# Spreading the expert weights: both halves of a weight in one 256-column matmul, summed by VectorE

## The reference, cut to what matters

```
s = einsum('nhpd,hpkd->nhpk', qry, sub_keys)
s_top, i_top = top_k(s, 16)
sc, ci = top_k(s_top[:, :, 0, :, None] + s_top[:, :, 1, None, :], 16)
experts = e_a * 128 + e_b          # e_a, e_b: the picked pair of key numbers
gw = softmax(sc)
out = sum over the picks of  gw * gelu(u[expert] . x) * v[expert]
```

## Time and profile before

| | us |
|---|---|
| median of 3 runs | 3646.55 (3645.39 to 3648.05) |
| the profiled execution, its own time | 3648.54 |
| its span, first to last instruction | 3646.8 |
| TensorE busy over the span | 3294.8 (90%) |
| VectorE busy | 1940.5 (53%) |
| ScalarE busy | 1114.6 (31%) |
| GpSimd busy | 1142.1 (31%) |
| mean granted TensorE clock | 0.939 |

### The profile page before, as it was taken

The page is one execution under the profiler, slowest core; times in us unless marked ns, Lnnn a source line. Parts: engine busy times, 40 slices in busy tenths (PEclk is TensorE's granted clock), DMA queues, the critical chain, the costliest instruction groups (busy, mean ns, idle before and its releaser), DMA issues. The chain is left out here.

```text
span 3646.8 us, 38847 instructions
## 1 busy us (share of the span) xinstructions
PE 3294.8 (90%) x15129; PEld 1668.3 (46%) x15390; DVE 1940.5 (53%) x2816; ACT 1114.6 (31%) x1609; POOL 1142.1 (31%) x545
## 2 busy tenths in 40 slices
PE   8678889999979899999999999999988877589897
PEld 3333347544644545464664444444433434234443
DVE  4772767543234675867770455555555442339631
ACT  3232234343323233342433333232333121232321
POOL 3311330133513243424223443444423001024332
PEclk9889999999989999999999999999999776599999
DMA  4101210122312244756577655565521000012321
GB/s 146 41 29 47 98 64 1 55 90 99 126 47 93 92 154 136 208 154 190 151 197 212 222 203 204 200 207 200 204 85 66 0 24 23 23 58 93 102 97 67
DMA packets 262822, 411.22 MB, mean 113 GB/s; under 512 B 146736, under 2 KB 146928, under 8 KB 262256
## 3 DMA queue, kind: packets, MB, share of 16 engines
q1 hardware_dynamic: 262640, 408.72, 34.3%
HBM read 339.45 MB, written 69.21 MB: 112 GB/s over the span
## 5 line engine op out<-in xcount | busy, mean ns | idle before, releaser
L498 POOL TENSOR_TENSOR weights_lo<-weights_as_loaded,weights_hi 128x1024 bf16<-128x1024 f32 x507 | 1112.5, 2196 | 2337.0 <-ACT weights_hi L494 2336.9
L494 ACT ACTIVATE weights_hi<-weights_as_loaded 128x1024 bf16<-128x1024 f32 x507 | 533.7, 1054 | 1185.2 <-PE banks L434 604.6
L1768 DVE TENSOR_TENSOR activation_lo<-activation_f,activation_hi 128x512 bf16<-128x512 f32 x128 | 278.9, 2179 | 313.0 <-ACT activation_hi L1660 313.0
L434 PE MATMUL banks<-normed_lo,weights_hi 128*128 128x512 bf16 x930 | 359.4, 386 | 27.0 <-PEq L296 15.8
L1581 PE MATMUL banks<-normed_hi,weights_hi 128*128 128x512 bf16 x991 | 376.6, 380 | 7.8 <-ACT gelu_out L1646 6.6
L1629 PE MATMUL banks<-activation_hi,weights_hi 128*128 128x512 bf16 x1004 | 380.8, 379 | 1.1
L1629 PE MATMUL banks<-activation_hi,weights_lo 128*128 128x512 bf16 x1003 | 380.4, 379 | 1.1
L1629 PE MATMUL banks<-activation_lo,weights_hi 128*128 128x512 bf16 x1003 | 380.4, 379 | 1.0
L1581 PE MATMUL banks<-normed_lo,weights_hi 128*128 128x512 bf16 x999 | 378.8, 379 | 1.7
L1581 PE MATMUL banks<-normed_hi,weights_lo 128*128 128x512 bf16 x1000 | 379.2, 379 | 1.3
L434 PE MATMUL banks<-normed_hi,weights_hi 128*128 128x512 bf16 x912 | 352.0, 386 | 29.5 <-PEq L277 20.2
(11 more groups left out here) (431 smaller groups left out, 4833.1 us busy)
## 6 DMA issues: line engine op xcount, KB each, us to landing
weights_as_loaded<-in_u_tiles SPq DMA_DIRECT2D x128, 512.0 KB, 3.9
weights_as_loaded<-in_v_tiles SPq DMA_DIRECT2D x128, 512.0 KB, 3.5
gelu_of_dots<-gelu_out SPq DMA_DIRECT2D x128, 256.0 KB, 2.2
activation_f<-gelu_of_dots SPq DMA_DIRECT2D x128, 256.0 KB, 3.7
expert_weight<-expert_weights SPq DMA_DIRECT2D x128, 256.0 KB, 4.0
expert_weights<-weight_grid_even SPq DMA_DIRECT2D x32, 512.0 KB, 5.9
expert_weights<-weight_grid_odd SPq DMA_DIRECT2D x32, 512.0 KB, 6.5
weights_as_loaded<-in_w_xbc SPq DMA_DIRECT2D x24, 512.0 KB, 3.5
```

Of the source, the lines that this page charges most:

```text
L434: ins = nc.tensor.matmul(self.ps[:, b, 0:tok], wk[:, s, k * P:(k + 1) * P], x[xk][:, g * 8 + k, :], start=first, stop=last)
L494: self.nc.scalar.activation(self.whi[:, s, :], self.wraw[:, s, :], ACT.Copy).then_inc(self.w_hi[s], 1)
L498: self.nc.gpsimd.tensor_tensor(self.wlo[:, s, :], self.wraw[:, s, :], self.whi[:, s, :], ALU.subtract).then_inc(self.w_lo[s], 1)
L1768: nc.vector.tensor_tensor(glo[:, j, :], gf[:, j, :], ghi[:, j, :], ALU.subtract).then_inc(S["g_lo"], 1)
```

## The change

One matmul of 256 columns makes both halves of a token. Its result is two runs of 128 in PSUM, which are no longer added up there. ScalarE copies the high run to the grid, and VectorE adds the low run to it (a new function `move` on VectorE, which signals `moved`; ScalarE now signals `hi_moved`). A group now fills all four banks, so `spread(g)` waits for the move of group g-1, half by half. `hotB` takes the layout of `hotA`, four tokens innermost, so its 128 key numbers lie 8 bytes apart as well. Groups follow as one, one, two over three slots in place of one, two over two; a block takes 12 slots in place of 11.

```
-    SPREAD_FROM = (30, 57, 85, 97)
-    TURN_AFTER = (22, 49, 76, 93)
-    EXP_AFTER = (13, 29, 57, 84)
+    SPREAD_FROM = (30, 58, 86, 98)
+    TURN_AFTER = (22, 52, 79, 95)
+    EXP_AFTER = (13, 29, 58, 86)
...
-                after[n] = min(left, 1 + n % 2)
+                after[n] = min(left, 1 + (n % 3 == 2))
...
-        hotB = self.sb("one_hot_b", [P, 2, G, P], BF16, ctx=tmp)
+        hotB = self.sb("one_hot_b", [P, 2, 2, P, 4], BF16, ctx=tmp)
-        hotAs = [self.sb("weighted_hot_a_" + n, [P, 2, 2, P, 4], BF16, ctx=tmp) for n in ("hi", "lo")]
+        hotAw = self.sb("weighted_hot_a", [P, 2, 2, 2, P, 4], BF16, ctx=tmp)
...
+        def halves(i):
+            return self.ps[:, 4 + 2 * i:6 + 2 * i, :].rearrange("p b (t w a) -> p (b t) w a", w=2, a=P)
...
                 def spread(g):
-                    if g < 2:
+                    if g == 0:
                         pe.wait_ge(S["copied"], TT)
-                    else:
-                        pe.wait_ge(S["moved"], 2 * (g - 1))
                     pe.wait_ge(S["hot"], g + 1)
                     for i in range(2):
+                        if g:
+                            pe.wait_ge(S["moved"], 2 * (g - 1) + i + 1)
                         for n in range(4):
-                            for m in range(2):
-                                ins = nc.tensor.matmul(self.ps[:, 4 + g % 2 * 2 + i, n * P:(n + 1) * P],
-                                                       hotB[:, g % 2, 4 * i + n, :], hotAs[m][:, g % 2, i, :, n],
-                                                       start=m == 0, stop=m == 1)
+                            ins = nc.tensor.matmul(self.ps[:, 4 + 2 * i + n // 2, n % 2 * 2 * P:(n % 2 + 1) * 2 * P].rearrange(
+                                                       "p (w a) -> p w a", a=P),
+                                                   hotB[:, g % 2, i, :, n], hotAw[:, g % 2, i, :, :, n], start=True, stop=True)
                         ins.then_inc(S["spread"], 1)
...
-                        nc.scalar.activation(grid[lap % 2][:, :, at + 4 * i:at + 4 * i + 4],
-                                             self.ps[:, 4 + g % 2 * 2 + i, :].rearrange("p (t a) -> p a t", a=P),
-                                             ACT.Copy).then_inc(S["moved"], 1)
+                        nc.scalar.activation(grid[lap % 2][:, :, at + 4 * i:at + 4 * i + 4].rearrange("p a t -> p t a"),
+                                             halves(i)[:, :, 0, :], ACT.Copy).then_inc(S["hi_moved"], 1)
...
+                def move(g):
+                    lap, at = g // 8, g % 8 * G
+                    for i in range(2):
+                        dve.wait_ge(S["hi_moved"], 2 * g + i + 1)
+                        cells = grid[lap % 2][:, :, at + 4 * i:at + 4 * i + 4].rearrange("p a t -> p t a")
+                        nc.vector.tensor_tensor(cells, cells, halves(i)[:, :, 1, :], ALU.add).then_inc(S["moved"], 1)
...
                     for k in range(PER):
                         one_hots(t, k)
+                        if k:
+                            move(t * PER + k - 1)
                         if t == 2 and k == PER // 2:
                             weigh_picks(3)
+                    move(t * PER + PER - 1)
```

More of the change, by code:

```diff
@@ L1494, in peer @@
         tot = self.sb("weight_sums", [P, PH], ctx=tmp)
-        iota_b = self.sb("iota", [P, P], BF16, ctx=tmp)
         iota_4 = self.sb("iota_fourfold", [P, P, 4], BF16, ctx=tmp)
@@ L1511, in peer @@
         S = {n: self.sem("peer_" + n) for n in ("keys", "scored", "copied", "shifted", "exped", "weights", "turned", "taken",
-                                               "hot", "spread", "moved", "weighed", "g_hi", "g_lo", "summed", "zeroed")}
+                                               "hot", "spread", "hi_moved", "moved", "weighed", "g_hi", "g_lo", "summed", "zeroed")}
         act_stored = [self.sem(f"gelu_stored{j}") for j in range(2)]
@@ L1750, in one_hots @@
                         dve.wait_ge(S["spread"], 2 * (g - 1))
-                    nc.vector.tensor_tensor(hotB[:, g % 2, :, :], iota_b[:, :].unsqueeze(1).to_broadcast((P, G, P)),
-                                            col[:, k * G:(k + 1) * G].unsqueeze(2).to_broadcast((P, G, P)), ALU.is_equal)
+                    nc.vector.tensor_tensor(hotB[:, g % 2, :, :, :], iota_4[:, :, :].unsqueeze(1).to_broadcast((P, 2, P, 4)),
+                                            four(col, k), ALU.is_equal)
                     link(nc.vector.tensor_tensor(hotA[:, :, :, :], iota_4[:, :, :].unsqueeze(1).to_broadcast((P, 2, P, 4)),
                                                  four(row, k), ALU.is_equal))
-                    nc.vector.tensor_tensor(hotAs[0][:, g % 2, :, :, :], hotA[:, :, :, :], four(whi, k), ALU.mult)
-                    link(nc.vector.tensor_tensor(hotAs[1][:, g % 2, :, :, :], hotA[:, :, :, :], four(wlo, k), ALU.mult))
+                    nc.vector.tensor_tensor(hotAw[:, g % 2, :, 0, :, :], hotA[:, :, :, :], four(whi, k), ALU.mult)
+                    link(nc.vector.tensor_tensor(hotAw[:, g % 2, :, 1, :, :], hotA[:, :, :, :], four(wlo, k), ALU.mult))
                     nc.vector.memset(spacer[:, :], 0.0).then_inc(S["hot"], 1)
+                def move(g):
[4 more added lines that the diff above has]
+                        nc.vector.tensor_tensor(cells, cells, halves(i)[:, :, 1, :], ALU.add).then_inc(S["moved"], 1)
                 def weigh(n):
@@ L1770, in _ @@
                 iota = self.consts[:, C_IOTA:C_IOTA + P]
-                nc.vector.tensor_copy(iota_b[:, :], iota)
                 link(nc.vector.tensor_copy(iota_4[:, :, :], iota.unsqueeze(2).to_broadcast((P, P, 4))))
```

## The result

The changed kernel takes 3736.8 us in the median of four runs (3734.3 to 3739.9), the kernel before 3647.0 beside it: a ratio of 1.0247, with an interval from 1.0229 to 1.0265. The forecast was 3688 with a range from 3650 to 3735. The direction was right, the size was half of what came, and the time lies just above the range. The profiled span grew from 3646.8 to 3732.5 us, and the mean granted clock fell from 0.939 to 0.927. Times are those of executions in the chip's usual state; one execution of run 1's kernel, its profiled one, ran at a mean granted clock of 0.562, took 5749.9 us and stands in no comparison.

What follows compares the result with a forecast made beforehand. TensorE's instructions bound the retrieval layer's first phase. -2 + 19 + 15 + 6 + 3 = +41 us on the profiled 3648.5 gives 3689.5, and 3688 as that run lay 2.0 above the median; range 3650 to 3735.

Steps and rivals of the forecast that it cites:

- the saving: TensorE's spread matmuls over 64 groups: 0 to 4.5 us less, taken as 2.
- a price of the columns' distance: Spread matmuls: 128 columns 8 bytes apart take the array 0.115 us, twice what contiguous ones take.
- The strided load: Weight load of `hotB`, now strided: even if twice as long, hidden under a matmul's 0.22 us, cost nothing.
- the new wait: Second group of a double slot waits for the first's moves, released by VectorE's addition: 16 x 1.2 = 19 us.
- The six late loads: Double slots 38, 65, 68, 95, 101, 107: late weight tiles delay ScalarE's moves, 6 x 2.4 = 15 us.
- the last block's start: Around slot 98, VectorE's one-hots and addition come late at the block boundary: 3 us (1 to 5).
- B: Spread matmuls: columns not slow, 256 take 0.109 us, kernel not slower: 3640 (3625 to 3652); chance 15%.
- C: Double slots: the wait doesn't bite as moves and second group's matmuls overlap better: 3645 to 3655; chance 5%.
- price of copy and addition: Moves in a double slot: ScalarE's first half 0.60 us, VectorE's additions 0.69 each, second group starting at 3.01.
- Rival A: Grid moves: addition or copy slow at 256 bytes between elements; 3706 at twice 0.69, 3761 at 2.18; chance 18%.
- The clock: TensorE at half clock after idle stretches of about 3.4 us, seven places, four counted: 6 us (0 to 11).
- off the path: VectorE's one-hots and additions, stretched where they meet GpSimd, fit beside TensorE's slots except at block starts.

Runs made afterwards that it cites:

- run 1: Changed kernel with ScalarE's copy and VectorE's addition walking the grid in runs of four neighbouring tokens: 3705.3 us, 1.016 of the kernel before.
- run 5: Kernel before with two tokens innermost in the moving operand, its columns 4 bytes apart in place of 8: 3599.3 us, 0.9869.
- run 6: Kernel before with only `hotB`, the stationary operand, in the change's layout, columns 8 bytes apart: 3653.0 us, 1.0014.
- run 4: Changed kernel with ScalarE's copies put ahead of its rounding of the next weight tile: 3703.2 us, 1.014.
- run 1 again: Second run, for a profile, of the changed kernel with copy and addition in runs of four tokens: 3710.6 us.
- run 10: Joined form: changed kernel with both spread operands 4 bytes apart, copy and addition in runs of four, copies ahead of rounding: 3618.8 us, 0.9917.

## Why the prediction came out half as large

**Right.** TensorE bounds the phase, and what is put between its instructions counts in full (86.1 us came up in this phase, 85.7 over the whole span). 256 columns take 0.229 us, forecast from 0.222 to 0.231, and the saving was 1.6 us, forecast 2. That rested on reading a price of the columns' distance out of the earlier trace rows against the earlier trace rows; run 5 confirms it. The strided load is hidden (run 6). The place and the releaser of the new wait are those named. The six late loads cost 17.3 us against 15, at the slots named, and the last block's start 3.7 against 3. Single slots lasted 7.0. Rivals B and C are out: the matmuls came 0.229 us apart and not 0.109, and the double slots waited.

**The step that failed** is the price of copy and addition under "The new wait": "ScalarE's first half ends at 1.64 + 0.60" and "0.69 each". Both were taken from rows in which the engine walks contiguous elements or runs of four, while the diff turns that walk round. Rival A named the cause and half of the price. It doubled the addition alone and got 3706; ScalarE's copy doubled too. With 1.07 and 1.29 the prediction's own sum gives 1.64 + 1.07 + 1.29 + 0.06 = 4.06 for the start of the second group, against the 4.12 measured, and with it 2.5 us a double slot in place of 1.2. Rival A's argument against itself, "no such price on ScalarE's writes", came from writes of four neighbours, which say nothing on single ones. Run 1 shows that the order alone makes the difference. The Trainium skill ("SBUF — State Buffer", Specifications (TRN2)) wants two hits in a memory line of 16 bytes for full bandwidth. These rows agree: 256 bytes apart is one hit and cost 1.8 to 1.9 times as much, runs of 16 bytes cost nothing.

**The clock** was the second miss, 23 us against 6. I counted places with about 3.4 us of idle time, since 1.51 had left the clock at 1.00 in the earlier trace rows. Stalls of 2.1 us were enough, and they stand in every double slot, so the price is not that of seven places but of sixteen. In part it grows with the first miss: with 1.62 us (run 4) the next slot took 7.5 to 9.1 nearly everywhere. But it was a miss of its own too. The prediction let a stall of its own length, about 1.1 us, cost nothing, and in run 1 again, which has that stall, the next slot was slower behind five of the seven undelayed double slots, up to 8.7. The clock as slot 32's second group starts, and behind it (columns as in the earlier trace rows):

```profile
1411.30:1412.30 1.00, 0.96 (x5) 0.55 (x6) 1.00 (x2) 0.00 (x0) 0.89 (x1) 0.99 1.01 369
1412.30:1415.70 3.40, 3.40 (x12) 1.29 (x11) 3.32 (x7) 1.19 (x2) 0.00 (x0) 0.50 0.05 16
```

In the joined form of run 10, with idle times of 1.08 us, the next slot kept its 6.09 everywhere. So the length of the idle time alone does not decide, and what else does stays open.

**Missed** altogether were slots 41 and 86, 4.7 us together. ScalarE in slot 86, then VectorE in slot 41:

```profile
1792.72 1.28 ACT L1672 ACT_TABLE_LOAD   x1
1794.01 0.31 ACT L1672 ACTIVATE picked<-picked 128x128 f32<-128x128 f32 x1
1794.23 1.87 ACT L1656 ACTIVATE weight_grid_even<-banks 128x512 f32<-128x512 f32 x2
```

```profile
1493.66 2.50 DVE L1756 TENSOR_TENSOR weighted_hot_a<-one_hot_a,pick_weight_hi 128x1024 bf16<-128x1024 bf16 x1
1496.08 0.68 DVE L1757 TENSOR_TENSOR weighted_hot_a<-one_hot_a,pick_weight_lo 128x1024 bf16<-128x1024 bf16 x1
1496.81 1.25 DVE L1765 TENSOR_TENSOR weight_grid_odd<-weight_grid_odd,banks 128x512 f32<-128x512 f32 x1
```

In 86 ScalarE takes an exponential with the load of its table (1.28 us) ahead of the copies, placed there by the change's own `EXP_AFTER`, for which the prediction had no term. In 41 the addition starts at 5.48 after the group, behind VectorE's one-hots, one of which takes 2.50 us in place of 0.69; the prediction had counted such a one off the path.

**The range** ended at 3735 because it took rival A half in. Rival A's sums made the stalls longer but left the clock at the forecast's 6 us, so the upper end was too low.

## To carry to other kernels

Price an operation by a row that has its access pattern, not only its shape: the same 512 elements cost 0.60 or 1.07 us on ScalarE, and a matmul's 128 columns 0.058 or 0.115, by the distance of neighbours alone. Before instructions are joined to save their number, see whether the number or the elements set their price; here a layout change gave what the joining could not. A wait put between TensorE's instructions costs its length and can then cost the clock (16 to 23 us here, in kernels whose stalls were 1.1 to 2.1 us), so when two engines' work comes to stand between two groups of matmuls, look first at how much other matmul work can stand there.

## What the runs showed of the hardware

- TensorE's moving operand in bf16: columns 8 bytes apart go at 0.115 us for 128 and 0.229 for 256, 4 bytes apart at 0.058 and 0.114, 2 bytes apart at 0.056 for 128. The Trainium skill's rule ("SBUF — State Buffer", Specifications (TRN2)) would let 8 bytes pass, as two elements fall into a line of 16. Here 8 bytes are half rate, so for this operand the measurement decides against it.
- Pairs of weight load and matmul follow each other at 0.058 us though a load lasts 0.096. A stationary operand 8 bytes apart adds 0.002 to pairs 0.116 apart.
- ScalarE's copy and VectorE's addition of 128x512 on the grid: 0.59 and 0.68 us in runs of 16 bytes, 1.07 and 1.29 at 256 bytes from element to element.
- VectorE's one-hot product over 128x1024 bf16 takes 1.22 us undisturbed when one weight is repeated along the innermost run of 128, 0.69 when two or four neighbouring weights stand innermost.
- 2.1 us without a matmul were followed by the lower granted clock in all seven undelayed double slots of the changed kernel, 1.1 us in five of seven places in run 1 again and in none of nine in the joined form of run 10. What else decides stays open.
